# Second mixer of the later layers: probabilities scaled and turned as the moving operand, sums split straight from PSUM

## The reference, cut to what matters

```python
q, k, v = jnp.split(x @ w_qkv, 3, axis=-1)          # [256, 1024] each
q = apply_rotary(split_heads(q, 8), inv_freq)        # rotary on 32 of 128 dims
k = apply_rotary(split_heads(k, 8), inv_freq)
s = jnp.einsum('bhqd,bhkd->bhqk', q, k) * dh ** -0.5 # causal mask
p = jax.nn.softmax(s, axis=-1)
o = jnp.einsum('bhqk,bhkd->bhqd', p, v)
return o.transpose(...).reshape(bsz, seq, nh * dh) @ w_out
```

## Time and profile before

| what | value |
|---|---|
| median of 3 runs | 1928.79 us |
| profiled execution | 1928.52 us |
| its span | 1926.7 us |
| PE busy | 1857.3 us, 96% |
| DVE, ACT busy | 917.1 us, 48%; 584.1 us, 30% |
| steps 0 to 17 of the mixer, to its first full output product | 1656.04 to 1716.65 us |
| in this stretch: PE busy | 56.74 of 60.61 us |
| granted PE clock there | 1.00 |

### The profile page before, as it was taken

One profiled execution on the slowest core, in us unless ns is written; L12 is line 12 of the kernel. 1 busy time (PEld: TensorE's weight loads), 2 busy tenths in 40 slices (PEclk: granted clock), 3 DMA queues, 4 the chain that ended last, 5 costly groups with the idle time before them and its releaser, 6 DMA issues.

```text
span 1926.7 us, 25464 instructions
## 1 busy us (share of the span) xinstructions
PE 1857.3 (96%) x10228; PEld 1110.0 (58%) x10228; DVE 917.1 (48%) x1607; ACT 584.1 (30%) x863; POOL 100.3 (5%) x120
## 2 busy tenths in 40 slices
PE   8999999999999999999999999999999999999998
PEld 5877874333333333233233333787888887878886
DVE  6864465323332333233232232676765455566544
ACT  3554442111111111111111111554435344555432
POOL 2410000000000000000000000020410000000000
PEclk9999999999999999999999999999999999999999
DMA  7543399999999999999999999542145455436452
GB/s 253 175 146 116 112 392 407 417 426 428 426 428 428 427 429 426 429 428 427 429 426 429 427 428 427 184 162 97 60 160 178 171 199 177 151 131 240 153 204 81
DMA packets 106464, 560.29 MB, mean 291 GB/s; under 512 B 5904, under 2 KB 11280, under 8 KB 81808
## 3 DMA queue, kind: packets, MB, share of 16 engines
q1 hardware_dynamic: 102528, 551.61, 71.2%
q10 hardware_dynamic: 3856, 7.53, 1.3%
HBM read 558.08 MB, written 1.05 MB: 290 GB/s over the span
## 4 chain that ended last, share of the span: by engine, by line
PE 71%; DMA 19%; DVE 4%; ACT 3%; issue 2%; POOL 1%; POOLq 0%; SPq 0%; ACTq 0%; DVEq 0%
PE ps L1297 14%; PE ps L948 11%; PE ps L949 11%; PE ps L950 11%; DMA ring<-in_w_gate_up_dram 10%; DMA arena<-in_w_gate_up_dram 8%; PE ps L1327 8%; PE ps L1226 2%; PE ps L1238 2%; PE ps L962 1%; PE ps L1312 1%; PE ps L1557 1%; DVE arena L2862 1%; PE ps L1434 1%; PE ps L984 1%
## 5 line engine op out<-in xcount | busy, mean ns | idle before, releaser
L1297 PE MATMUL ps<-ring,arena 128*64 128x512 f32 x1280 | 286.6, 596 | 23.8 <-DMA ring<-in_w_gate_up_dram 23.8
L2720 DVE TENSOR_SCALAR arena<-ps 128x512 f32<-128x512 f32 x32 | 22.1, 691 | 518.5 <-PE ps L1297 518.5
L2260 DVE TENSOR_TENSOR split_w<-ring,split_w 128x1024 fp32r<-128x1024 f32 (+2 forms) x176 | 203.9, 1205 | 81.9 <-ACT split_w L2054 81.3
L948 PE MATMUL ps<-split_w,act_parts 128*128 128x512 f32 (+1 forms) x544 | 209.7, 386 | 2.0 <-issue 1.0
L1297 PEld LDWEIGHTS ps<-ring,arena 128*64 128x64 f32 x1280 | 87.8, 137 | 209.9 <-issue 161.5
L950 PE MATMUL ps<-split_w,act_parts 128*128 128x512 f32 (+1 forms) x544 | 205.7, 378 | 0.0
L949 PE MATMUL ps<-split_w,act_parts 128*128 128x512 f32 (+1 forms) x544 | 205.3, 377 | 0.0
L2054 ACT ACTIVATE split_w<-ring 128x1024 fp32r<-128x1024 f32 (+2 forms) x176 | 171.7, 1033 | 110.1 <-PE ps L950 108.6
L1297 PE MATMUL ps<-arena 128*64 128x512 f32 x768 | 172.5, 595 | 10.6 <-DMA arena<-in_w_gate_up_dram 10.3
L1327 PE MATMUL ps<-ring,arena 128*64 128x512 f32 x720 | 160.6, 594 | 0.1
L1945 ACT ACTIVATE arena<-arena 128x512 f32<-128x512 f32 x32 | 20.2, 630 | 457.7 <-DVE arena L2720 457.7
(11 more groups left out here) (382 smaller groups left out, 2804.3 us busy)
## 6 DMA issues: line engine op xcount, KB each, us to landing
ring<-in_w_gate_up_dram SPq DMA_DIRECT2D x80, 2048.0 KB, 34.1
arena<-in_w_gate_up_dram SPq DMA_DIRECT2D x48, 2048.0 KB, 27.0
ring<-in_w_down_dram SPq DMA_DIRECT2D x45, 2048.0 KB, 33.7
ring<-in_f_w_dram SPq DMA_DIRECT2D x28, 2048.0 KB, 8.0
arena<-in_w_down_dram SPq DMA_DIRECT2D x19, 2048.0 KB, 37.2
ring<-in_w_in_dram SPq DMA_DIRECT2D x14, 2048.0 KB, 7.8
ring<-in_a_w_in_dram SPq DMA_DIRECT2D x6, 2048.0 KB, 8.1
ring<-in_b_w_qkv_dram SPq DMA_DIRECT2D x6, 2048.0 KB, 8.0
```

Of the source, the lines that this page charges most:

```text
L948: pe.matmul(dst, lh, rh, start=start, stop=False)
L1297: mm = pe.matmul(ps[half, bank, :], xeT[:, 2 * c + j, :], w[:, j, col:col + 512], start=False, stop=(c == 3 and j == 1), skip_group_check= ...
L2260: dve.tensor_tensor(part_place(load, 1, k, n)[:, s_, :], raw_place(load, k, n)[:, s_, :], part_place(load, 0, k, n)[:, s_, :], ALU.subtract)\
L2720: dve.tensor_scalar(gate_c, ps[:, 1, :], 7.0, None, ALU.min).then_inc(m_clipped, 1)
```

## The change

The operands of the weighted sum change places: v is stationary and the turned probabilities move. The result then has the head's 128 features on the partitions and the queries in the columns, which is how the output product wants its stationary operand. So:

- The division can't be done per partition behind the sum any more. It is moved ahead of the turning: DVE takes the reciprocal and multiplies the probabilities in SBUF with it (new semaphore `mb_scaled`). PE's turning of unit i - 1 waits for `mb_scaled` where it waited for `mb_probs`, and so does the exponential two units on (before: `mb_inverted`).
- The high and low part of the output are made right from PSUM per unit, 128x128: ACT copies (new, `mb_high`), DVE subtracts (in the place of the division's L3175), into `oT_m`.
- The `early` events and the turning behind the list go: 4 groups of four turnings on PE, 4 copies of 128x512 on ACT, 4 subtractions of 128x512 on DVE. The output product waits per head for `mb_o`.
- `oT_m` lies where the rows of the first norm lay; for this layer they are loaded to another place (`ln_rows[2]`). One semaphore of the first layer (`gd_soft`) is merged into another.

```diff
@@ PE
             def turned_wait(first, tile, k):
-                if k % 4 == 0:
-                    at = tile + 2 * (k // 4) if first == TURN_MOBA_OUT else 2 * tile + k // 4
-                    pe.wait_ge(turn_done, first + at + 1)
+                if first is None:
+                    pe.wait_ge(mb_o, 2 * k + tile + 1)
+                elif k % 4 == 0:
+                    pe.wait_ge(turn_done, first + 2 * tile + k // 4 + 1)
...
                         for kt in range(tile + 1):
-                            mm = pe.matmul(ps[:, 7, 0:P], probsT_m[:, kt * P:(kt + 1) * P],
-                                           v_m[:, kt, h * P:(h + 1) * P], start=(kt == 0),
+                            mm = pe.matmul(ps[:, 7, 0:P], v_m[:, kt, h * P:(h + 1) * P],
+                                           probsT_m[:, kt * P:(kt + 1) * P], start=(kt == 0),
                                            stop=(kt == tile))
                     if 0 <= i - 1 < MOBA_UNITS:
                         u = i - 1
-                        pe.wait_ge(mb_probs, u + 1)
+                        pe.wait_ge(mb_scaled, u + 1)
...
-            pe.wait_ge(mb_o, MOBA_UNITS)
-            for tile in range(NT):
-                four(5 + 2 * tile, lambda j: o_m[:, tile, 512 + j * P:512 + (j + 1) * P])\
-                    .then_inc(turned, 1)
@@ ACT
                     i = event[1]
+                    if 0 <= i - 2 < MOBA_UNITS:
+                        h, tile = divmod(i - 2, 2)
+                        act.wait_ge(mb_pv, i - 1)
+                        act.activation(oT_m[:, 0, h, tile * P:(tile + 1) * P], ps[:, 7, 0:P],
+                                       ACT.Copy).then_inc(mb_high, 1)
                     if i < MOBA_UNITS:
...
-                            act.wait_ge(mb_inverted, i - 1)
+                            act.wait_ge(mb_scaled, i - 1)
@@ DVE
                     i = event[1]
+                    u = i - 1
+                    if 0 <= u < MOBA_UNITS:
+                        dve.wait_ge(mb_probs, u + 1)
+                        inv, x = inv_m[:, u % 2:u % 2 + 1], probs_m[:, u % 2, 0:(u % 2 + 1) * P]
+                        after(step.on(dve.reciprocal(inv, sum_m[:, u % 2:u % 2 + 1])))
+                        dve.tensor_scalar(x, x, inv, None, ALU.mult).then_inc(mb_scaled, 1)
                     if i < MOBA_UNITS:
...
-                        dve.wait_ge(mb_pv, u + 1)
-                        dve.wait_ge(mb_inverted, u + 1)
-                        dve.tensor_scalar(o_m[:, tile, h * P:(h + 1) * P], ps[:, 7, 0:P],
-                                          inv_m[:, u % 2:u % 2 + 1], None, ALU.mult)\
-                            .then_inc(mb_o, 1)
...
+                        dve.wait_ge(mb_high, u + 1)
+                        dve.tensor_tensor(oT_m[:, 1, h, s_], ps[:, 7, 0:P], oT_m[:, 0, h, s_],
+                                          ALU.subtract).then_inc(mb_o, 1)
```

More of the change, by code:

```diff
@@ L230 @@
 TURN_GDN = 16
-TURN_LN1 = [20, 32]
-TURN_MOBA_IN, TURN_MOBA_OUT = 24, 28
+TURN_LN1 = [20, 28]
+TURN_MOBA_IN = 24
 RAW_SLOTS = (1, 0)
@@ L374, in moba_timeline @@
             events.append(("split", LOAD_MOBA + c + 1, 2 * tile + 1))
[L375 to L378, removed]
     pieces = [(0, 0, 0, 2), (0, 0, 2, 4), (1, 0, 0, 2), (1, 0, 2, 4)]
@@ L669, in program @@
         junk_o, junk = area(14336, D), area(13312, D)
-        ln_rows = [area(15872, 2, D), rows[:, :].rearrange("p (a n) -> p a n", a=2)]
+        ln_rows = [area(15872, 2, D), rows[:, :].rearrange("p (a n) -> p a n", a=2),
+                   area(8192, 2, D)]
         ln_gained = area(14336, D)
@@ L1384, in tok, with mixed_rows @@
                 return lambda k: (act_high[:, k, s_], act_low[:, k, s_])
+            def mixed_rows(tile):
+                s_ = slice(tile * P, (tile + 1) * P)
+                return lambda k: (oT_m[:, 0, k, s_], oT_m[:, 1, k, s_])
             for tile in range(NT):
@@ L1605, in mixer_out @@
                             at = (2, lambda: turn_normed(4 * layer))
-                        second(g + 2 * tile + n, tok(tile), load + n, KD, 512, (first, tile), at,
-                               ks)
+                        second(g + 2 * tile + n, (mixed_rows if layer else tok)(tile), load + n,
+                               KD, 512, (first, tile), at, ks)
             mixer_out(G_GDN_OUT, LOAD_GDN_OUT, TURN_GDN, 0, lambda: turn_gated(1))
@@ L1733, in _ @@
                         mm.then_inc(mb_pturned, 1)
[L1734 to L1739, removed]
-                    four(3, lambda j: o_m[:, tile, j * P:(j + 1) * P]).then_inc(turned, 1)
                 elif event[0] == "out":
                     _, tile, n, k0, k1 = event
-                    second(G_MOBA_OUT + 2 * tile + n, tok(tile), LOAD_MOBA_OUT + n, KD, 512,
-                           (TURN_MOBA_OUT, tile), None, (k0, k1))
-            pe.wait_ge(mb_o, MOBA_UNITS)
-            for tile in range(NT):
-                four(5 + 2 * tile, lambda j: o_m[:, tile, 512 + j * P:512 + (j + 1) * P])\
-                    .then_inc(turned, 1)
-            mixer_out(G_MOBA_OUT, LOAD_MOBA_OUT, TURN_MOBA_OUT, 1, None)
+                    second(G_MOBA_OUT + 2 * tile + n, mixed_rows(tile), LOAD_MOBA_OUT + n, KD, 512,
+                           (None, tile), None, (k0, k1))
+            mixer_out(G_MOBA_OUT, LOAD_MOBA_OUT, None, 1, None)
             feed_forward(1)
@@ L2133, in feed_forward @@
                     cast_load(load)
-            def out_high(tile, b, bank):
-                act.wait_ge(turned, TURN_MOBA_OUT + 2 * b + tile + 1)
-                act.activation(act_high[:, 4 * b:4 * b + 4, tile * P:(tile + 1) * P],
-                               ps[:, bank, :].rearrange("p (k n) -> p k n", n=P), ACT.Copy)\
-                    .then_inc(act_high_done, 1)
             def mixer_norm(layer):
@@ L2175, in _ @@
             ln_squares(3)
-            ln_load(0, "ln1_g_2", "ln1_b_2", 1)
+            ln_load(2, "ln1_g_2", "ln1_b_2", 1)
             turn_high(TURN_MOBA_IN, 1)
@@ L2225, in _ @@
                         act.activation(probsT_m[:, 0:n], ps[:, 6, 0:n], ACT.Copy).then_inc(mb_pt, 1)
-            for tile in range(NT):
-                out_high(tile, 1, 5 + 2 * tile)
             mixer_norm(1)
```

42 lines of the change are left out of this document (11 added, 31 removed).

## The result

The changed kernel takes 1935.05 us (median of 10 runs, 1933.34 to 1937.66), the one before took 1929.53 in the same session (10 runs, 1928.77 to 1931.05): ratio 1.0026, 95% interval 1.0018 to 1.0035, 5.5 us slower. The forecast was +5.4 us, and the range 1931.6 to 1937.0. The profiled execution took 1935.53 us, with a span of 1933.7.

A forecast was written before the change was run, and what follows sets the result against it. PE, busy 96% of the span, was taken to bound the kernel. Terms +5.8 - 0.9 + 1.2 + 1.3 - 2.0 gave +5.4 us on the 1928.8 median: 1934.2 us, range 1931.6 to 1937.0.

The forecast's parts named there:

- The ring: Steps 0 to 9: PE, DVE and ACT wait on each other; pair of steps 9.0 us, not 7.61; +5.8 us.
- The scaling's price: DVE's multiplication of probabilities in SBUF: 0.35 us for a 256-wide unit, 0.29 for a 128-wide one.
- the rate from PSUM: Upper bound for DVE's multiplication: 0.89 ns a column, 0.35 and 0.46 us, whole change +6.5 us.
- The lower bound: DVE's multiplication takes no more than a reciprocal, 0.15 us for either width; whole change +3.2 us.
- The early turnings: Two groups of four turnings on PE ahead of step 10 are gone: -0.9 us.
- the tail: Behind the list, from the first of eight last turnings to the first matmul behind them: -2.0 us.
- the short steps: Steps 11 to 17: little product on PE to hide the longer way from exponential to turning; +1.3 us.
- Step 10: DVE's longest queue: PE stands 3.1 us and turns unit 9 some 3.5 us into the step; net +1.2 us.
- PE's waits for the scaling: Sign: about 1.2 us in odd steps, 0.2 in even, some 3 in step 10; under 5 us total means wrong.
- Too small to tell: Rival: whole change only +2 to +3.8 us, pair of steps 8.6 to 8.8 us, 1932.3 us; chance 0.15.
- Faster: Rival: PE never comes to stand at the scaling in the mixer's steps; 1925.9 us; chance 0.05.
- The clock: Rival: PE's clock falls to half in the 3.1 us wait of step 10; about 1938 us; chance 0.05.

The follow-up runs named there:

- Division moved alone: Kernel before, with only reciprocal and multiplication put first in the next step and PE's turning waiting for them: 1938.90 us, ratio 1.0040 against the kernel before.
- no division: Changed kernel without reciprocal and multiplication, PE waiting only for the exponentials, mixer not computed: 1926.87 us, ratio 0.9985 against the kernel before.
- The second session: Changed kernel measured again, unaltered, against the kernel before: 1935.19 us against 1929.15, ratio 1.0035, interval 1.0026 to 1.0045.

## Why the prediction was right

The stages, from scores to scores on PE, in the changed kernel run again (no fall in step 10), against before. "Steps 0 to 8" ends at the scores of step 8, and step 8 itself, the same in both, stands in the sum alone:

| stage | before | changed | difference | predicted |
|---|---|---|---|---|
| steps 0 to 8 | 30.64 | 36.73 | +6.1 | +5.8 |
| step 9, early turnings gone | 7.38 | 6.60 | -0.8 | -0.9 |
| steps 10 and 11 | 6.45 | 7.57 | +1.1 | +1.2 |
| steps 12 to 14 | 5.80 | 6.90 | +1.1 | +1.3, as 11 to 17 |
| 15 to the norm | 17.33 | 15.42 | -1.9 | -2.0 |
| sum with step 8 | 71.12 | 76.72 | +5.6 | +5.4 |

- *The ring.* Right. A pair was put at 9.0 and is 9.14. The 0.14 is 0.07 in PE's part (3.24, not 3.17) and the rest in gaps between engines: 0.08 from ACT's copy to the rotary part and 0.06 from the scaling to the turning, where 0.04 was taken. The turning comes later behind the scores than before by 1.23 us in the odd step and by 0.18 in the even one, predicted 1.2 and 0.2. "Division moved alone" shows that the loss is this and no other part.
- *The scaling's price.* 354 and 287 ns, predicted 0.35 and 0.29. That line was drawn through two rows read from SBUF, 0.52 ns a column, and the two shapes here give 0.52 again; the rate from PSUM, 0.89, is refuted for this place. The rule of the Trainium skill, "VectorE: DVE Perf Modes", section on the 2×_2P mode, that a float32 `tensor_scalar` in SBUF uses both read ports agrees. The lower bound, +3.2 with only the wait and the reciprocal, measured some +2.6.
- *The early turnings, the tail, the short steps.* The table mixes them with the division's cost; "no division" parts them. There step 9 is 0.9 us shorter than before, as predicted, and the part from step 15 to the norm 2.1 shorter, predicted 2.0. The division adds 1.1 in steps 12 to 14 and 0.2 behind them, together the 1.3 predicted.
- *Step 10.* The turning came 3.52 us into the step, predicted 3.5; the sum of unit 9 5.62 into it, predicted 5.6. Only the stand is split: 0.56 for ACT's copy ahead of the sum, 2.12 for the scaling, 2.7 and not 3.1 in all. What the copy takes, the scaling's wait gives back.
- *PE's waits for the scaling*: 7.2 us. Less than 5 would have shown the mechanism wrong.
- *Too small to tell* isn't excluded by the first interval: its lower end, 1.0018, is 3.5 us, within that rival's +2 to +3.8. The second session's interval begins at 1.0026, and the pair is 9.14 us, not the 8.6 to 8.8 that the rival needs. So it falls, by the pair more than by the time. *Faster* falls; it comes true only with the scaling in another place.
- *The clock* was misjudged. "So 3.1 us should pass" rested on the earlier trace rows, where the granted clock stood at 1.00 through 4 us of idleness at the kernel's end. That one stretch at the end says nothing reliable of a stand in the middle: in 4 of 6 profiles the clock fell in or behind the wait of step 10, whose longest piece was 1.7 to 2.7 us. A chance of 0.05 was too low. The price, some 4 us, let 3 to 5 us of PE's work run at half the clock, for which no row was given. It was too high: the clock was back at 1711.6, and the fall took 1.6 us and gave 0.5 back. In the first profile it is the difference between the +5.6 of the table and +6.7. In the layer before this one it falls behind still shorter waits, but the one profile of the kernel before doesn't have that fall, so no row could warn of it. The rule of the Trainium skill, "TensorE: Matmul & The Clock Gate", "HAM oscillation", that waits between bursts can drop the clock was nearer than my row.

The rest of the first profile's 7.0 us of span, 0.3, lies ahead of the mixer: 1.65 us more behind the clock's fall in the layer before, and 1.3 less ahead of that, where the code is the same but for the merged semaphore. In how many of the unprofiled runs the clock fell, at either place, stays open. So the mechanism and its size are shown by the stretch, 5.6 us without falls; that the medians differ by 5.5, only 0.1 from the forecast, is in part luck.

## What to carry to other kernels

An operation put in front of a wait costs by its place in the queue more than by its length: two reciprocals and two scalings, 0.95 us together, made a pair of steps 1.5 us longer behind the weight quarters, and cost nothing in a gap where their engine waited anyway. When an edit makes the bound engine wait for one that is half idle, walk the ring of waits through all engines once round and compare it with the bound engine's own step; then look for the gap in that ring, and put the operation there. Price a new stand of the matrix engine with a possible fall of its clock, and look at several profiles of the same kernel, and at the granted clock along all of each, not only where the change is.

## What the runs showed of the hardware

- The same kernel with the same stand, 0.56 and 2.12 us, held the clock at 1.00 in two profiles, and in one it fell to the lower level, 0.50 (1.2 GHz), from 1708.2 to 1711.6 us.
- The clock also fell to 0.50 in the mixer of the layer before, in 8 of 13 profiles, where PE's single waits were 0.74 us at most. It cost 1.4 to 1.7 us, in three of them 2.5 to 2.8.
- A fall of PE's clock gives part of its cost back where PE waits for other engines soon after: 0.54 of 1.61 us.
- A DVE multiplication in SBUF by a constant is 59 to 60 ns shorter than by a value per partition: 294 against 353 ns for 128x256, 227 against 286 for 128x128.
